# Stick-breaking attention: the causal table written into the scores by VectorE instead of added by TensorE

## The chip, the core and the metric

The kernel runs on one core of one Trainium2 chip. The metric is the device time of one execution in microseconds. TensorE (PE, with its weight loads as PEld), VectorE (DVE), ScalarE (ACT), GpSimd (POOL) and SyncE (SP) run their own instruction streams and wait for each other by semaphores.

## What is computed

Two transformer-like layers on 1024 tokens of width 1024 in float32. The first layer has a stick-breaking attention of 8 heads of width 128, a chunkwise retention of 4 heads, gates and projections; the second has gated linear attention, sliding-window attention and a feed-forward part. The change touches the stick-breaking attention alone:

```python
def block(args):                       # one tile of 128 queries
    z = einsum('bhqd,bhkd->bhqk', qi, k) * scale
    mask = kpos[None, :] < qpos[:, None]
    log_keep = where(mask, log_sigmoid(-z), 0.0)
    suffix = cumsum(log_keep, axis=3, reverse=True) - log_keep
    w = where(mask, exp(log_sigmoid(z) + suffix), 0.0)
    return einsum('bhqk,bhkd->bhqd', w, v)
```

## The kernel before

The program is one long sequence written by hand for each engine, without a scheduler: what an engine does next is the order of the lines in its block, and semaphores tie the engines together. The 30 projections come first (to about 653 us), then the stick-breaking attention (to about 1024 us), then branch projections, retention and the second layer.

**The attention stage.** `sb_pair(i, n)` runs for i = 0 to 3, each a pair of heads, and stands once in each engine's block. A pair has 16 steps S. `step(S)` gives head `c = S % 2` and a tile of 128 queries; `step_w(S)` gives the width, the keys up to and with the tile's own block. Even steps grow (S=0: 128, 2: 256, ... 14: 1024), odd steps shrink (S=1: 1024, 3: 896, ... 15: 128). The scores of step S lie in two PSUM banks, 4 and 5 or 6 and 7 by turns. One step goes over the engines so:

- PE `scores(S)`: the product of queries and keys in float32, up to 512 columns at a time (L2684; the trace shows each as two records), then on the last 128 columns the product of identity and table in fp32r (L2686), which adds -1e30 where a key isn't before its query. Then `z_done`. It first waits for `z_used` of step S-2, as the banks are shared.
- DVE `clamp(S)`: the smaller of score and 40 into `L` (L1943), then `m_ready`.
- ACT `softplus_terms(S)`: exp of L (L1343), relu of score less 40 into R (L1344), between them and the next the copy of the transposes of step S-2 (L1354), then a drain and ln of L (L1348), then `l_ready`.
- DVE `suffix_sum(S)`: scan from the right over L + R into C (L1951); `score_less_sum(S)`: a drain (L1956), then score less C into C (L1957), then `z_used`.
- ACT: exp of C (L1373), then `wgt`.
- PE `turn(S)`: transposes of C (L2695). ACT (L1354) and DVE (L1918) copy them out; `weigh` multiplies them with the values every two tiles (L2666), and DVE keeps that product (L1924).

The steps overlap. In iteration S VectorE runs: subtraction of S, copies of S-1 and of the values product, at S = 4, 5, 12, 13 half a weight block's low part (L1909), scan of S+1, clamp of S+2. ScalarE runs: exp of C for S, at times the copy of a gate product (L1365), the terms of S+2 with the copy for S inside. TensorE runs: the scores of S+2, part of the filler, the transposes of S, at some steps the values product, the rest of the filler. The filler (L2710) is the gate's projection in 512-column products, dealt out over the steps by a table (`fill_upto`), to give TensorE work while the chain of one step goes over the other engines. `end_of_pair` multiplies by the gate (L1936). Behind the last pair come the products of L593.

Near the kernel's start GpSimd loads the table `causal` by DMA, and ScalarE rounds it and the identity to fp32r (L1246, L1247), in place and into `ident_r`. PE waits for that before the stage (L2651).

Of the kernel before, what the change touches and what calls it, by code (L numbers as in the profile page):

```python
# [6 lines left out]
P = 128  # L7
KT = DM // P
TT = SEQ // P
# [50 lines left out]
def build(nc, x, norm_gain, w_in, b_merge, sb_q_gain, sb_k_gain, ret_out_gain, w_branch_sb, w_branch_ret, w_out,  # L60
          meta_tokens_2, norm_mix_w_2, w_in_2, w_gate_up_2, b_gate_2, gla_norm_w_2, sinks_2, w_out_2,
          norm_ff_w_2, w_ff1_2, w_ff2_2, final_norm_w_2, tab, out):
    f32, f32r, i32 = mybir.dt.float32, mybir.dt.float32r, mybir.dt.int32
    ACT, ALU, AX = mybir.ActivationFunctionType, mybir.AluOpType, mybir.AxisListType
# [5 lines left out]
    def at(name, shape, dt=f32, off=None):  # L70
        size = int(np.prod(shape[1:])) * 4
        o = cur[0] if off is None else off
        t = nc.alloc_sbuf_tensor_at(name, shape, dt, offset=o)
        if off is None:
            cur[0] += size
        return t

    ident = at("ident", [P, P])
# [21 lines left out]
    pos = [0]  # L100

    def work(name, shape, dt=f32):
        t = at(name, shape, dt, off=pos[0])
        pos[0] += int(np.prod(shape[1:])) * 4
        assert pos[0] <= work_end, (name, pos[0] - work_end)
        return t
# [29 lines left out]
    Q = work("q", [P, 2, SEQ])  # L136
    K = work("k", [P, 2, SEQ])
# [4 lines left out]
    WT = [work(f"wt{u}", [P, TT, 2 * P]) for u in range(2)]  # L142
    stage = [work(f"stage{u}", [P, HALF]) for u in range(2)]
    causal = work("causal", [P, P])
    causal_r = at("causal_r", [P, P], f32r, off=pos[0] - P * 4)
    ident_r = work("ident_r", [P, P], f32r)

    pos[0] = work_at
    S_hi = work("s_hi", [P, KT, SEQ], f32r)
# [96 lines left out]
    with ctx:  # L246
# [3 lines left out]
        def wide(b, w=SEQ):  # L250
            return ps[:, b:b + 2, :].rearrange("p a b -> p (a b)")[:, 0:w]
# [7 lines left out]
        const_in, const_ok = sem("constants_in"), sem("constants_ok")  # L259
# [356 lines left out]
        n1_hi, n1_lo, own_gain = sem("norm1_hi_and_raw_and_mask"), sem("norm1_lo"), sem("gain_in")  # L616
# [9 lines left out]
        z_done, m_ready, l_ready, z_used = sem("z_done"), sem("z_clamped"), sem("softplus_ready"), sem("z_used")  # L626
# [4 lines left out]
        causal_in = sem("causal_in")  # L631
# [540 lines left out]
        def _(act):  # L1172
# [68 lines left out]

            first_block(0)
            first_block(1)
            act.wait_ge(causal_in, 16)
            act.wait_ge(const_in, 16 * (1 + len(spec)))
            act.activation(causal_r[:, :], causal[:, :], ACT.Copy)  # L1246
            act.activation(ident_r[:, :], ident[:, :], ACT.Copy).then_inc(n1_hi, 1)  # L1247
            first_block(2)
            token_sum_hi(2, 4)
            first_block(3)  # L1250
# [521 lines left out]
        def _(dve):  # L1772
# [99 lines left out]
            for n in range(1, NPROJ + 1):  # L1872
# [17 lines left out]
                y, z = PC[out_tile(n, 3)][:, :], PC[out_tile(n, 2)][:, :]  # L1890
# [47 lines left out]
            def sb_pair(i, n):  # L1938

                def clamp(S):  # L1940
                    w = step_w(S % 16)
                    dve.wait_ge(z_done, 16 * i + S + 1)
                    dve.tensor_scalar(L[S % 2][:, 0:w], wide(4 + 2 * (S % 2), w), CLAMP, None, ALU.min).then_inc(m_ready, 1)  # L1943

                def suffix_sum(S):

                    w = step_w(S % 16)
                    dve.wait_ge(l_ready, 16 * i + S + 1)
                    if 16 * i + S >= 2:
                        dve.wait_ge(tr_done, 16 * i + S - 1)  # L1950
                    dve.tensor_tensor_scan(C[S % 2][:, 0:w][:, ::-1], L[S % 2][:, 0:w][:, ::-1], R[S % 2][:, 0:w][:, ::-1], 0.0, ALU.add, ALU.add)  # L1951

                def score_less_sum(S):

                    w = step_w(S)
                    dve.drain()  # L1956
                    dve.tensor_tensor(C[S % 2][:, 0:w], wide(4 + 2 * (S % 2), w), C[S % 2][:, 0:w], ALU.subtract).then_inc(z_used, 1)  # L1957

                if i == 0:
                    clamp(0)  # L1960
                    clamp(1)
                    suffix_sum(0)
                for S in range(16):
                    if S != 1 or i == 0:
                        score_less_sum(S)
                    if S - 2 in pair_after:
                        keep_attended(i, pair_after[S - 2])
                    if S >= 1:
                        keep_second(i, S - 1)
                    elif i:  # L1970
                        keep_attended(i - 1, 6)
                        keep_second(i - 1, 15)
                    if S in (4, 5):
                        half_lo(n + 1, 1, S - 4)
                    if S in (12, 13):
                        half_lo(n + 2, 0, S - 12)
                    if i < 3 or S < 15:
                        suffix_sum(S + 1)
                    if S == 0 and i:
                        score_less_sum(1)  # L1980
                        end_of_pair(i - 1)
                    if i < 3 or S < 14:
                        clamp(S + 2)
                if i == 3:
                    keep_attended(3, 6)
                    keep_second(3, 15)

            for i in range(4):
                sb_pair(i, L1 + 2 * i)
            end_of_pair(3)  # L1990
# [567 lines left out]
        def _(pe):  # L2558
# [70 lines left out]
            for n in range(1, NPROJ):  # L2629
# [18 lines left out]
                    pe.wait_ge(t_dve, 10)  # L2648
                product(n, 5)
                product(n, 6)  # L2650
            pe.wait_ge(n1_hi, TT + 5)  # L2651

            def weigh(i, q):

# [15 lines left out]
            def sb_pair(i, n):  # L2670

                def scores(S):
                    c, qt = step(S % 16)
                    w = step_w(S % 16)
                    if S % 16 == 0:
                        pe.wait_ge(qk_in, 32 * (i + S // 16) + 32)
                    if S % 16 == 1:
                        pe.wait_ge(v_in, 48 * (i + S // 16) + 32)
                    if 16 * i + S >= 2:
                        pe.wait_ge(z_used, 16 * i + S - 1)  # L2680
                    for h in range(0, w, HALF):
                        e = min(w, h + HALF)
                        z = wide(4 + 2 * (S % 2))[:, h:e]
                        pe.matmul(z, Q[:, c, qt * P:(qt + 1) * P], K[:, c, h:e], start=True, stop=(e < w))  # L2684
                    z = wide(4 + 2 * (S % 2))[:, w - P:w]
                    pe.matmul(z, ident_r[:, :], causal_r[:, :], start=False, stop=True).then_inc(z_done, 1)  # L2686

                def turn(S):
                    pe.wait_ge(wgt, 16 * i + S + 1)
                    if i or S:  # L2690
                        pe.wait_ge(wt0, 16 * i + S)
                    if i or long_steps(S):
                        pe.wait_ge(wt1, 8 * i + long_steps(S))
                    for kb in range(step(S)[1] + 1):
                        last = pe.transpose(wide(0)[:, kb * P:(kb + 1) * P], C[S % 2][:, kb * P:(kb + 1) * P], ident[:, :])  # L2695
                    last.then_inc(tr_done, 1)

                def filler(first, upto):

                    for m in range(first, upto):  # L2700
                        J, r = divmod(m, PASSES)
                        b, j = divmod(J, 4)
                        th, ct = j // 2, j % 2
                        k, g = divmod(r, 3)
                        if r == 0 and (i or J):
                            pe.wait_ge(g_raw, 8 * i + J)
                        if r == 0 and j == 0:
                            pe.wait_ge(w_lo, n + (1 + b))
                        w, a = ((W_hi, A_hi), (W_hi, A_lo), (W_lo, A_hi))[g]
                        last = pe.matmul(bank[3], w[b][:, k, ct * P:(ct + 1) * P], a[:, k, th * HALF:(th + 1) * HALF],  # L2710
                                         start=(r == 0), stop=(r == PASSES - 1))
                        if r == PASSES - 1:
                            last.then_inc(gp_done, 1)

                if i == 0:
                    scores(0)
                    scores(1)
                    pe.wait_ge(*v_kept(NPROJ - 1))
                else:
                    weigh(i - 1, 7)  # L2720
                for S in range(16):
                    first, upto = fill_upto[S - 1] if S else 0, fill_upto[S]
                    early = first if S - 1 in fill_after else upto if S == 0 else (first + upto) // 2
                    if S == 0:
                        filler(first, early)
                    if i < 3 or S < 14:
                        scores(S + 2)
                    if S:
                        filler(first, early)
                    elif i == 0:  # L2730
                        pe.wait_ge(*c_kept(NPROJ - 1, 3))
                    turn(S)
                    if S - 1 in pair_after:
                        weigh(i, pair_after[S - 1])
                    filler(early, upto)
# [534 lines left out]
```

## Time and profile before

| | |
|---|---|
| median of 3 runs | 2576.06 us (2573.29 to 2579.47) |
| the profiled execution | 2574.54 us |
| its span | 2572.8 us |
| PE busy | 2476.6 us, 96% |
| DVE busy | 1585.9 us, 62% |
| ACT busy | 1078.1 us, 42% |
| POOL busy | 213.3 us, 8% |
| chain that ended last | PE 79%, DVE 8%, ACT 5%, DMA 3% |

The span is what the trace covers; 1.7 us lie around it. Busy time of TensorE counts overlapping, pipelined products, whose ends are modelled; so the starts of two neighbouring products tell what one costs, and its printed duration doesn't. "Idle before" in brackets behind a row of the timeline is the time in which that engine had nothing to run, and what ended it.

### The profile page before, as it was taken

Reading aid. Unit: us, or ns where it says so; the run is one execution under the profiler, and the core shown is the slowest. Engines: PE = TensorE matmul, PEld = TensorE weight load, DVE = VectorE, ACT = ScalarE, POOL = GpSimd, SP = SyncE. Lnnn points to the kernel's source line nnn. Section 1 sums busy time; section 2 is a strip of 40 time slices with the busy share of each in tenths; the row PEclk is TensorE's granted clock in tenths of the full one; section 3 lists DMA queues with packets and bytes.
Section 4 is the critical chain, followed back from the end, with each engine's and each line's share of the span. In section 5 each row is a group of like instructions: output and inputs, shape, how many; then the busy total and the mean of one; then the engine's idle time right before and its main releaser. Section 6 shows DMA issues by size and latency. Waiting matters only on the chain.

```text
span 2572.8 us, 30810 instructions
## 1 busy us (share of the span) xinstructions
PE 2476.6 (96%) x12198; PEld 2016.7 (78%) x12198; DVE 1585.9 (62%) x2033; ACT 1078.1 (42%) x1749; POOL 213.3 (8%) x351
## 2 busy tenths in 40 slices
PE   6999999999899999999999999999999999999997
PEld 5777888888677777878788776887777888888886
DVE  7666556555566665366652556046737776788779
ACT  6454322233566666322421436134525444443333
POOL 0001111111000000100011003000001211200000
PEclk9999999999999999999999999999999999999999
DMA  4222333333221121634133310110143444583432
GB/s 141 90 80 97 98 127 103 98 103 133 79 92 62 57 80 50 232 115 178 37 98 128 115 49 18 50 34 17 60 130 107 143 154 154 198 298 141 157 127 102
DMA packets 139145, 278.49 MB, mean 108 GB/s; under 512 B 16765, under 2 KB 91178, under 8 KB 132218
## 3 DMA queue, kind: packets, MB, share of 16 engines
q1 hardware_dynamic: 109354, 176.52, 20.7%
q0 software_dynamic: 29648, 100.00, 11.0%
q8 instruction: 97, 1.59, 0.3%
q14 instruction: 46, 0.38, 0.1%
HBM read 196.79 MB, written 79.69 MB: 107 GB/s over the span
## 4 chain that ended last, share of the span: by engine, by line
PE 79%; DVE 8%; ACT 5%; DMA 3%; DVEq 2%; issue 2%; ACTq 1%; SPq 0%; POOL 0%
PE ps L2612 32%; PE ps L593 11%; PE ps L3242 8%; PE ps L2862 6%; PE ps L2710 4%; PE ps L2666 2%; PE ps L587 2%; PE ps L2684 2%; PE ps L3136 1%; DVE c L1951 1%; PE ps L2926 1%; PE ps L2620 1%; PE ps L2847 1%; PE ps L2695 1%; PE ps L3121 1%
## 5 line engine op out<-in xcount | busy, mean ns | idle before, releaser
L1870 DVE TENSOR_TENSOR proj_out<-ps,proj_out 128x512 f32<-128x512 f32 x292 | 195.9, 686 | 253.5 <-PE ps L2612 248.2
L2612 PE MATMUL ps<-a_hi,pw_hi 128*128 128x512 f32 x528 | 213.7, 405 | 0.8 <-ACT proj_out L1234 0.8
L2612 PE MATMUL ps<-a_lo,pw_hi 128*128 128x512 f32 x528 | 205.8, 390 | 0.0
L2612 PE MATMUL ps<-t_hi,pw_hi 128*128 128x512 f32 x464 | 188.5, 406 | 0.0
L2612 PE MATMUL ps<-t_lo,pw_hi 128*128 128x512 f32 x464 | 180.9, 390 | 0.0
L573 DVE TENSOR_TENSOR w_lo<-w_raw,w_hi 128x2048 fp32r<-128x2048 f32 x28 | 64.1, 2289 | 124.1 <-ACT w_hi L569 118.7
L2612 PE MATMUL ps<-a_hi,pw_lo 128*128 128x512 f32 x352 | 137.6, 391 | 0.0
L569 ACT ACTIVATE w_hi<-w_raw 128x2048 fp32r<-128x2048 f32 x28 | 53.6, 1913 | 164.9 <-DMA w_raw<-in_w_out 65.8
L1951 DVE TENSOR_TENSOR_SCAN c<-l,r 128x128 f32<-128x128 f32 (+7 forms) x64 | 86.8, 1356 | 57.3 <-ACT l L1348 57.2
L2612 PEld LDWEIGHTS ps<-a_hi,pw_hi 128*128 128x128 f32 x528 | 99.1, 188 | 24.8 <-issue 5.0
L2612 PEld LDWEIGHTS ps<-a_lo,pw_hi 128*128 128x128 f32 x528 | 99.2, 188 | 23.8 <-issue 3.8
L1815 DVE TENSOR_TENSOR pw_lo<-pw_raw,pw_hi 128x512 fp32r<-128x512 f32 x176 | 113.1, 684 | 0.1
L3242 PE MATMUL ps<-ws_hi,hidden_hi 128*128 128x512 f32 x288 | 112.2, 390 | 0.5 <-DVE a_plain L2505 0.5
L3242 PE MATMUL ps<-ws_lo,hidden_hi 128*128 128x512 f32 x288 | 112.1, 389 | 0.0
L3242 PE MATMUL ps<-ws_hi,hidden_lo 128*128 128x512 f32 x288 | 112.1, 389 | 0.0
L2710 PE MATMUL ps<-a_hi,w_hi 128*128 128x512 f32 x256 | 107.8, 421 | 3.0 <-DVE w_lo L573 2.9
L1198 ACT ACTIVATE pw_hi<-pw_raw 128x512 fp32r<-128x512 f32 x132 | 73.5, 621 | 86.3 <-DMA pw_raw<-in_w_in 43.3
L2612 PEld LDWEIGHTS ps<-t_lo,pw_hi 128*128 128x128 f32 x464 | 87.2, 188 | 21.3 <-issue 3.8
L2612 PEld LDWEIGHTS ps<-t_hi,pw_hi 128*128 128x128 f32 x464 | 87.2, 188 | 21.2 <-issue 3.8
L2862 PE MATMUL ps<-w_hi,a_hi 128*128 128x512 f32 x256 | 102.1, 399 | 0.0
L2710 PE MATMUL ps<-a_hi,w_lo 128*128 128x512 f32 x256 | 101.8, 398 | 0.0
L2710 PE MATMUL ps<-a_lo,w_hi 128*128 128x512 f32 x256 | 101.0, 395 | 0.0
(493 smaller groups left out, 6598.6 us busy)
## 6 DMA issues: line engine op xcount, KB each, us to landing
pw_raw<-in_w_in SPq DMA_DIRECT2D x30, 1024.0 KB, 5.8
hidden_raw<-hidden_forms SPq DMA_DIRECT2D x28, 1024.0 KB, 4.8
projections<-proj_out POOLq DMA_DIRECT2D x88, 256.0 KB, 3.4
w_raw<-in_w_in SPq DMA_DIRECT2D x18, 1024.0 KB, 5.2
pw_raw<-in_w_ff SPq DMA_DIRECT2D x16, 1024.0 KB, 6.3
w_quarter<-in_w_ff SPq DMA_DIRECT2D x16, 1024.0 KB, 7.1
hidden_forms<-proj_out POOLq DMA_DIRECT2D x56, 256.0 KB, 3.5
hidden_forms<-nb POOLq DMA_DIRECT2D x56, 256.0 KB, 3.4
```

The source lines that it names most:

```text
L569: act.activation(W_hi[s][:, :, :], W_raw[s][:, :, :], ACT.Copy).then_inc(w_hi, 1)
L573: dve.tensor_tensor(W_lo[s][:, :, :], W_raw[s][:, :, :], W_hi[s][:, :, :].bitcast(f32), ALU.subtract).then_inc(w_lo, 1)
L587: last = pe.matmul(bank[banks[j]][:, r * BC:(r + 1) * BC], a[:, k, t:t + P], w[s][:, k, :], start=(k == 0 and g == 0), stop=(k == KT - 1 a ...
L593: last = pe.matmul(bank[banks[j]][:, :], w[s][:, k, ct * P:(ct + 1) * P], a[:, k, th * HALF:(th + 1) * HALF], start=(k == 0 and g == 0), s ...
L1198: last = act.activation(PWH[s][:, q, :, :], raw_part(s, q), ACT.Copy)
L1815: last = dve.tensor_tensor(lo_part(s, q), raw_part(s, q), PWH[s][:, q, :, :].bitcast(f32), ALU.subtract)
L1870: return dve.tensor_tensor(out_ap(n, j), product_bank(n, o), src, ALU.add)
L1951: dve.tensor_tensor_scan(C[S % 2][:, 0:w][:, ::-1], L[S % 2][:, 0:w][:, ::-1], R[S % 2][:, 0:w][:, ::-1], 0.0, ALU.add, ALU.add)
L2612: last = pe.matmul(product_bank(n, o), w, a[:, k0 + k, t], start=(k == 0 and g == 0), stop=(k == 3 and g == 2))
L2710: last = pe.matmul(bank[3], w[b][:, k, ct * P:(ct + 1) * P], a[:, k, th * HALF:(th + 1) * HALF], start=(r == 0), stop=(r == PASSES - 1))
L2862: last = pe.matmul(bank[row_bank(t)], a[:, kk, tok], half_rows(w[s])[:, k, :], start=(s == 0 and k == 0 and g == 0), stop=(s == 1 and k == ...
L3242: last = pe.matmul(bank[4 * ((g + 1) % 2) + t], a[u][:, k, tok], w[u][:, k, :], start=(k == 0 and v == 0), stop=(k == 3 and v == 2))
```

## The change

VectorE waits once for the table ahead of the stage. Ahead of each clamp it now copies the table into the last 128 score columns in PSUM, where the table is not zero (the table's own bits are the predicate), and drains. TensorE's product of identity and table is gone, and the last product of the scores counts up `z_done`. The two ScalarE copies and TensorE's wait for them are gone, with the tiles `causal_r` and `ident_r`. The whole diff:

```diff
--- before.py
+++ after.py
@@ -142,8 +142,6 @@
     WT = [work(f"wt{u}", [P, TT, 2 * P]) for u in range(2)]
     stage = [work(f"stage{u}", [P, HALF]) for u in range(2)]
     causal = work("causal", [P, P])
-    causal_r = at("causal_r", [P, P], f32r, off=pos[0] - P * 4)
-    ident_r = work("ident_r", [P, P], f32r)
 
     pos[0] = work_at
     S_hi = work("s_hi", [P, KT, SEQ], f32r)
@@ -1241,10 +1239,6 @@
 
             first_block(0)
             first_block(1)
-            act.wait_ge(causal_in, 16)
-            act.wait_ge(const_in, 16 * (1 + len(spec)))
-            act.activation(causal_r[:, :], causal[:, :], ACT.Copy)
-            act.activation(ident_r[:, :], ident[:, :], ACT.Copy).then_inc(n1_hi, 1)
             first_block(2)
             token_sum_hi(2, 4)
             first_block(3)
@@ -1940,6 +1934,8 @@
                 def clamp(S):
                     w = step_w(S % 16)
                     dve.wait_ge(z_done, 16 * i + S + 1)
+                    dve.copy_predicated(wide(4 + 2 * (S % 2))[:, w - P:w], causal[:, :].bitcast(i32), causal[:, :])
+                    dve.drain()
                     dve.tensor_scalar(L[S % 2][:, 0:w], wide(4 + 2 * (S % 2), w), CLAMP, None, ALU.min).then_inc(m_ready, 1)
 
                 def suffix_sum(S):
@@ -1985,6 +1981,7 @@
                     keep_attended(3, 6)
                     keep_second(3, 15)
 
+            dve.wait_ge(causal_in, 16)
             for i in range(4):
                 sb_pair(i, L1 + 2 * i)
             end_of_pair(3)
@@ -2648,7 +2645,6 @@
                     pe.wait_ge(t_dve, 10)
                 product(n, 5)
                 product(n, 6)
-            pe.wait_ge(n1_hi, TT + 5)
 
             def weigh(i, q):
 
@@ -2681,9 +2677,8 @@
                     for h in range(0, w, HALF):
                         e = min(w, h + HALF)
                         z = wide(4 + 2 * (S % 2))[:, h:e]
-                        pe.matmul(z, Q[:, c, qt * P:(qt + 1) * P], K[:, c, h:e], start=True, stop=(e < w))
-                    z = wide(4 + 2 * (S % 2))[:, w - P:w]
-                    pe.matmul(z, ident_r[:, :], causal_r[:, :], start=False, stop=True).then_inc(z_done, 1)
+                        last = pe.matmul(z, Q[:, c, qt * P:(qt + 1) * P], K[:, c, h:e], start=True, stop=True)
+                    last.then_inc(z_done, 1)
 
                 def turn(S):
                     pe.wait_ge(wgt, 16 * i + S + 1)
```

## Rows read from the trace of the kernel before

**Rows 1.** Busy by stretch: A:B, us, PE, PEld, DVE, ACT, POOL, clock, DMA, GB/s.
```profile
834.00:924.00 90.00, 86.36 (x411) 67.41 (x410) 57.96 (x72) 59.10 (x98) 2.25 (x5) 1.00 0.22 71
```

**Rows 2.** Who waited for whom, 834 to 924 us: total us, times, longest.
```profile
PE ps L2695 <- ACT c L1373: 2.9, 4, 1.2
```

**Rows 3.** Timeline (start, us, engine, line, tiles, [idle before]), pair's start to the scores of S=5.
```profile
851.80 0.43 DVE L1943 TENSOR_SCALAR l<-ps 128x256 f32<-128x256 f32 x1 [0.77 <-PE ps L2686]
...
854.25 1.07 DVE L1943 TENSOR_SCALAR l<-ps 128x896 f32<-128x896 f32 x1
...
854.61 1.09 PE L2695 MATMUL ps<-ident,c 128*128 128x128 f32 x8 [1.17 <-ACT c L1373]
...
858.66 2.02 DVE L1951 TENSOR_TENSOR_SCAN c<-l,r 128x896 f32<-128x896 f32 x1 [2.23 <-ACT l L1348]
...
860.60 0.53 DVE L1943 TENSOR_SCALAR l<-ps 128x384 f32<-128x384 f32 x1
...
861.23 1.09 DVE L1957 TENSOR_TENSOR c<-ps,c 128x896 f32<-128x896 f32 x1
...
862.38 1.13 PE L2684 MATMUL ps<-k,q 128*128 128x512 f32 x2 [0.17 <-DVE c L1957]
```

**Rows 4.** Timeline, to the transposes of S=7.
```profile
874.20 0.42 DVE L1924 COPY out_t<-ps 128x256 f32<-128x256 f32 x1 [2.71 <-PE ps L2666]
...
881.72 0.80 DVE L1943 TENSOR_SCALAR l<-ps 128x640 f32<-128x640 f32 x1
...
885.87 0.77 PE L2695 MATMUL ps<-ident,c 128*128 128x128 f32 x5 [0.40 <-ACT c L1373]
```

**Rows 5.** Timeline, to the transposes of S=11.
```profile
898.87 0.53 DVE L1943 TENSOR_SCALAR l<-ps 128x384 f32<-128x384 f32 x1
...
901.47 0.96 DVE L1951 TENSOR_TENSOR_SCAN c<-l,r 128x384 f32<-128x384 f32 x1 [1.02 <-ACT l L1348]
...
902.60 1.09 DVE L1943 TENSOR_SCALAR l<-ps 128x896 f32<-128x896 f32 x1 [0.17 <-PE ps L2686]
...
907.47 0.55 PE L2695 MATMUL ps<-ident,c 128*128 128x128 f32 x3 [0.88 <-ACT c L1373]
```

**Rows 6.** Timeline, S=14 to the next pair's first scores.
```profile
913.13 1.23 DVE L1943 TENSOR_SCALAR l<-ps 128x1024 f32<-128x1024 f32 x1 [0.52 <-PE ps L2686]
...
920.23 0.27 DVE L1943 TENSOR_SCALAR l<-ps 128x128 f32<-128x128 f32 x1
...
920.59 1.23 DVE L1957 TENSOR_TENSOR c<-ps,c 128x1024 f32<-128x1024 f32 x1
...
921.96 0.46 PE L2684 MATMUL ps<-k,q 128*128 128x128 f32 x2 [0.51 <-DVE c L1957]
```

**Rows 7.** Groups by line, 650 to 1060 us: busy us, mean ns, idle before.
```profile
L2686 PE MATMUL ps<-causal_r,ident_r 128*128 128x128 f32 x64 | 30.1, 470 | 0.0
```

**Rows 8.** Timeline of TensorE at S=6.
```profile
868.07 1.02 PE L2684 MATMUL ps<-k,q 128*128 128x512 f32 x2
...
868.50 0.59 PE L2684 MATMUL ps<-k,q 128*128 128x512 f32 x1
...
869.27 0.40 PE L2710 MATMUL ps<-a_lo,w_hi 128*128 128x512 f32 x1
...
869.50 0.39 PE L2710 MATMUL ps<-a_hi,w_lo 128*128 128x512 f32 x1
```

**Rows 9.** Groups by line and shape on VectorE: ns min/median/max; busy us, mean ns.
```profile
L2209 DVE COPY_PREDICATED ss<-window,ps x14: 731/746/749, 1538.1 to 1588.1; 128x512 f32<-128x512 int32 x14
...
L1957 DVE TENSOR_TENSOR c<-ps,c 128x512 f32<-128x512 f32 x2 | 1.4, 692 | 0.2
...
L1957 DVE TENSOR_TENSOR c<-ps,c 128x128 f32<-128x128 f32 x2 | 0.6, 292 | 0.2
```

**Rows 10.** Busy TensorE by stretch at the stage's start: PE, granted clock.
```profile
668.00:670.00 2.00, 0.00 (x0) 0.86 0.00 0
...
674.00:676.00 2.00, 2.00 (x11) 0.50 0.00 0
```

## The prediction

> **What bounds the kernel now.** I began with the page's busy shares and its chain: TensorE is busy for 96% of the span and holds 79% of the chain that ended last, while VectorE is busy for 62%. Taken alone that speaks for the change, since it takes work from the busiest engine. But a share is a mean over stages, and the change lies in one, the attention of four head pairs between 653 and 1024 us. The second view is the busy time by stretch. One pair takes about 90 us; in it TensorE is busy 86.4 us, VectorE 58.0 and ScalarE 59.1, at a full granted clock [rows 1]. TensorE is nearly full, but not quite, and the question of this case is what ends its idle time.
>
> The third view is who waited for whom in one pair. TensorE's transposes (L2695) waited 2.9 us in four places for ScalarE's exp of the weights (L1373) [rows 2]. These places are not noise: they come back at the same steps in each of the pairs. The fourth view, the timeline, shows what stands behind each. I name a step by S (0 to 15 in a pair); each goes scores (PE L2684, L2686), clamp (DVE L1943), exp, relu, ln (ACT), scan (DVE L1951), subtraction (DVE L1957), exp (ACT L1373), transposes (PE L2695). TensorE covers this latency with the gate product (L2710) and the values product (L2666), but not wholly:
> - Behind the pair's start it waits 1.17 us at the transposes of S=1 (854.61) and 0.17 us at the scores of S=5 (862.38) [rows 3].
> - 0.40 us at the transposes of S=7 (885.87) [rows 4].
> - 0.88 us at the transposes of S=11 (907.47) [rows 5].
> - 0.51 us at the next pair's first scores (921.96) [rows 6], and once more right behind them, at the transposes of S=14, which wait for the exp of the same difference.
>
> At these places TensorE isn't the bound; the chain through VectorE and ScalarE is, and VectorE's clamp, where the change adds its work, lies in it.
>
> **What is removed.** 64 products of identity and table [rows 7]. The mean of 470 ns in that row is a pipelined latency, not a cost; starts tell the cost. The scores of S=6 are two records, the first starting at 868.07 and the second at 868.50, so 0.43 us each, and they would be through by 868.93. A 512-column gate product takes 0.23 us from start to start (869.27 to 869.50), so the second one behind the scores would start at 868.93 + 0.23 = 869.16 if nothing lay between. It starts at 869.27 [rows 8]. One L2686 ahead of the gate product thus costs TensorE 0.11 us. Ahead of transposes, which are short themselves, I take about half, 0.06, an estimate. If TensorE were the bound everywhere, 64 of them would give back 4 to 7 us; that is the change's ceiling. The two ScalarE copies near the kernel's start lie beside VectorE's sums of the token halves, for which ScalarE waits right behind them, so I cost them at nothing; if that cover were gone they would be worth two operations of about 0.3 us, the size of the 128x128 row in [rows 9]. The wait of TensorE for them (L2651) and the new wait of VectorE for the table are long fulfilled at 650 us: nothing. SyncE's waits on the count of finished scores move with TensorE.
>
> **What is added.** Ahead of each clamp, on VectorE, one predicated copy of 128x128 into the scores, and a drain. No row shows this shape, nor a VectorE write to PSUM. The kernel's own predicated copies are 128x512 and take 746 ns, where a subtraction of 128x512 takes 692 and one of 128x128 takes 292 [rows 9]. That is (692-292)/384 = 1.04 ns an element, so 746 - 384 x 1.04 = 346 ns for the new one. The bounds: not under the 0.27 us of the clamp of 128x128 (920.23) [rows 6], which reads one tensor where the copy reads two, and not over 746 ns, the large one. I take 0.35 us, nearest to the row of its own kind. The drain is read off the neighbours: a clamp without one in front begins 0.08 us before the scan ahead of it ends (858.66 + 2.02 = 860.68 against 860.60), the subtraction behind a drain begins 0.10 us after the clamp ends (860.60 + 0.53 = 861.13 against 861.23) [rows 3]. The clamp now comes behind such a drain, so each step's clamp ends c = 0.35 + 0.09 = 0.44 us later (0.36 to 0.84 by the bounds).
>
> These rows show that an explicit drain costs 0.10 + 0.08 = 0.18 us of overlap [rows 3]. The Trainium skill (VectorE: DVE Perf Modes, "The DRAIN you can't avoid") says that the pipe is emptied after every VectorE operation anyway, so that chaining operations saves nothing. By that rule the explicit drain would be free; the trace speaks against it, and the sum goes by the rows.
>
> VectorE's own load stays far from the bound: 58.0 + 16 x 0.44 = 65 us in a pair of over 90 [rows 1]. What counts is how often c is in the chain between two places where TensorE has the lead. Pair by pair, on the rows of the pair from 834 to 924:
> - Pair start to the scores of S=5 [rows 3]. Scores of S=2, clamp of S=2 (851.80), exp, relu, ln, scan of S=2, clamp of S=3 (854.25), exp, relu, ln, scan of S=3 (858.66), clamp of S=4 (860.60), which stands ahead of the subtraction of S=3 (861.23), and the scores of S=5 wait for that (862.38). Three clamps: 3c. TensorE is already idle before it, so there is no slack. The 1.17 us at S=1 is inside: ScalarE's queue holds the exp of S=1 behind the ln of S=2, so it grows by 1c.
> - Values product to the transposes of S=7 [rows 4]. VectorE keeps the attended rows when that product is done (874.20), splits a weight block, scans S=6, then clamps S=7, and after the scan of S=7 clamps S=8 (881.72); the exp of S=7 stands behind S=8's terms on ScalarE. 2c.
> - Values product to the transposes of S=11 [rows 5]. From VectorE's copy of it over the clamps of S=11 (898.87) and S=12 (902.60). The scan between ends at 901.47 + 0.96 = 902.43, so by the overlap of 0.08 the clamp of S=12 could have begun at 902.35, some 0.26 us earlier than it does; it was TensorE's scores that it waited for. 2c - 0.26.
> - Scores of S=14 to the next pair [rows 6]. Clamp of S=14 (913.13), scan, clamp of S=15 (920.23), subtraction (920.59), scores of the next pair (921.96). 2c.
>
> Sum 9c - 0.26 = 3.70 us a pair. Against it stand the removed products that lie where TensorE leads: S=5 and 6 (0.18), S=10 (0.12), S=14 (0.06, since the scores are announced earlier), and the next pair's S=1 and 2 (0.18): 0.54 us. The others end in a place where TensorE then waits anyway. Net 3.16 us a pair, and four pairs, since the first pair's start has the same three clamps on its way (there inside TensorE's wait of [rows 10]) and the last ends the same way: +12.6 us. Behind the stage TensorE leads alone and the shift stays.
>
> **The sum.** The profiled run took 2574.5 us (span 2572.8), so it becomes 2587.1. It is 1.5 us below the median of the three; I put the forecast between 2587.1 and 2576.1 + 12.6 = 2588.7, at 2588.
>
> **The rivals.**
> - *TensorE is the bound after all (faster).* If VectorE's extra 0.44 us went into its own idle time everywhere, the 64 products of 0.06 to 0.11 us would come off, some 5 us: about 2571 us. For it: VectorE idles a third of the pair. Against it: TensorE's waits stand behind these very clamps. It decides only if c is below 3.2/36 = 0.09 us, since 36c - 3.2 is the balance; the shortest VectorE row is three times that. 4%.
> - *Largely absorbed (within 0.2%).* A shorter copy and a free drain (c near 0.2) and part of the nine clamps hidden behind ScalarE, whose queue orders several of the exps: about 2579. 9%.
> - *A free drain.* If the drain costs nothing beside a copy this short, c is 0.35 - 0.08 = 0.27 us, the balance 36 x 0.27 - 3.2 = 6.5 us, the time 2581 us from the profiled run's own. Against it: the 0.10 us behind the drain in [rows 3]. This is what the Trainium skill's rule above would give. 9%.
> - *The forecast.* c between 0.3 and 0.5 at nine clamps a pair: 2582 to 2591. 61%.
> - *A dearer copy.* If writing PSUM under a predicate costs as much as the large copy (c = 0.84) the balance is 36 x 0.84 - 3.2 = 27, 2603 us; halfway, c = 0.6, it is 18, 2594 us. At such c further places with under 1 us to spare (the scores of S=9, S=12 and S=14) begin to wait too. 10%.
> - *The clock.* At the stage's very start TensorE has no product at all from 668 to 670 us, and then runs at half clock, 1.2 GHz, still from 674 to 676 [rows 10]. The waits inside the pairs (up to 1.17 us) have left the clock at 1.00 [rows 1]. They grow to 1.7 us, and at the pair's end to some 2 us in two parts. If one such place a pair brought the clock down as there, each would cost up to half of some 6 us, 12 us in all on top of the 12.6: 2600 us. 7%.
>
> **Range and chances.** 2581 to 2595 leaves out the first two cases and half of the last two, about 2 in 10. The likeliest alone is 2585 to 2591. A change of under 0.2% (5 us) can't be told from none in this kernel, whose three runs lie 6 us apart. The free drain lies on that edge, and I count a third of it as within. Faster 4%, within 12%, slower 84%.
>
> **What would show it.** In the changed kernel: a new VectorE group of 64 predicated copies of about 350 ns; the clamp beginning 0.09 us after each; a pair's period of about 93 us instead of 90; TensorE's waits in a pair about doubled, at the same steps as before (1.6 at S=1; 1.0 at S=5; 0.40 + 2c + 0.18 for the two products that fall away on TensorE's side = 1.5 at S=7; 0.88 + 0.62 + 0.18 = 1.7 at S=11); a granted clock of 1.00; the stretches ahead of 653 and behind 1024 of the same length. A period of 88 to 89 would overthrow the chain; a period of 93 with another length of copy would mean that the count of clamps is wrong; a clock under 1.00 inside pairs would be the last rival.

## The result and the profile after

The changed kernel takes 2587.96 us in the median of its runs, against 2577.32 for the kernel before in the same comparison: ratio 1.0040, 95% interval 1.0027 to 1.0054. Measured once more beside the experiments it is 2587.34 against 2576.22, ratio 1.0048, interval 1.0033 to 1.0063. The change costs 10 to 11 us. One of the seven runs in the first comparison took 8491.07 us at a mean granted clock of 0.407, and the ratio leaves it out; without it the median is 2587.1. The profiled execution took 2584.05 us.

The first lines of its page, span and busy time by engine:

```profile
span 2582.3 us, 30807 instructions
PE 2470.1 (96%) x12134; PEld 2005.0 (78%) x12134; DVE 1604.3 (62%) x2097; ACT 1078.6 (42%) x1747; POOL 212.8 (8%) x351
```

TensorE has 64 products less and is busy 6.5 us less; VectorE has 64 operations more and is busy 18.4 us more; the span is 9.5 us longer. Nothing in these lines says that the trade is bad, except the span. In the changed file the copy is L1937, the clamp L1939, the scan L1947, the subtraction L1953, the scores L2680, the transposes L2690, the gate product L2705.

One pair of heads in the middle of the stage, as the busy time of one stretch (to set beside [rows 1]), the copies as a group by line with busy time and mean ns, and who waited for whom in that stretch (to set beside [rows 2]; the last fence has the waits at the scores before):

```profile
838.00:930.60 92.60, 85.34 (x392) 65.09 (x392) 62.58 (x89) 59.17 (x99) 2.16 (x4) 1.00 0.20 68
```

```profile
L1937 DVE COPY_PREDICATED ps<-causal 128x128 f32<-128x128 int32 x64 | 18.2, 285 | 22.0 <-PE ps L2680 21.6
```

```profile
PE ps L2690 <- ACT c L1367: 4.8, 4, 1.6
...
PE ps L2680 <- DVE c L1953: 2.4, 2, 1.4
```

```profile
PE ps L2684 <- DVE c L1957: 0.7, 2, 0.5
```

The pair takes 92.60 us in place of 89.91. TensorE's busy time in it fell by 1.0 us, and its waits at the transposes grew from 2.9 us to 4.8 [rows 2], those at the scores from 0.7 us to 2.4: 3.6 us of waits became 7.2. VectorE is busy 62.6 us of 92.6, far from full. The work taken off TensorE turned into waiting.

I measure a pair by the subtraction of S=14, the one of width 1024 that closes it, at the ends of the second and the third pair. Before, the later one starts at 920.59 [rows 6] and the earlier one here, 89.91 us ahead of it:

```profile
830.68 1.23 DVE L1957 TENSOR_TENSOR c<-ps,c 128x1024 f32<-128x1024 f32 x1
```

After:

```profile
837.99 1.23 DVE L1953 TENSOR_TENSOR c<-ps,c 128x1024 f32<-128x1024 f32 x1
...
930.59 1.23 DVE L1953 TENSOR_TENSOR c<-ps,c 128x1024 f32<-128x1024 f32 x1
```

The timeline of the stretch that [rows 3] shows of before, from the scores of S=2 to those of S=5:

```profile
858.98 0.30 DVE L1937 COPY_PREDICATED ps<-causal 128x128 f32<-128x128 int32 x1 [1.10 <-PE ps L2680]
859.35 0.42 DVE L1939 TENSOR_SCALAR l<-ps 128x256 f32<-128x256 f32 x1
...
861.20 0.69 DVE L1947 TENSOR_TENSOR_SCAN c<-l,r 128x256 f32<-128x256 f32 x1 [1.42 <-ACT l L1342]
861.80 0.28 DVE L1937 COPY_PREDICATED ps<-causal 128x128 f32<-128x128 int32 x1
...
862.15 1.09 DVE L1939 TENSOR_SCALAR l<-ps 128x896 f32<-128x896 f32 x1
862.16 1.09 PE L2690 MATMUL ps<-ident,c 128*128 128x128 f32 x8 [1.61 <-ACT c L1367]
...
868.53 0.27 DVE L1937 COPY_PREDICATED ps<-causal 128x128 f32<-128x128 int32 x1
...
868.88 0.56 DVE L1939 TENSOR_SCALAR l<-ps 128x384 f32<-128x384 f32 x1
...
869.53 1.09 DVE L1953 TENSOR_TENSOR c<-ps,c 128x896 f32<-128x896 f32 x1
...
870.68 0.70 PE L2680 MATMUL ps<-k,q 128*128 128x512 f32 x1 [1.02 <-DVE c L1953]
```

Before, the clamp of S=3 begins (854.25) some 0.08 us before the scan in front of it ends (853.64 + 0.69 = 854.33). Now the copy stands in that place (861.80, the scan ends at 861.89) and the clamp comes 0.35 us later (862.15). Three such copies lie on the way to the scores of S=5, and TensorE waits there 1.02 us instead of 0.17, at the transposes of S=1 1.61 us instead of 1.17 [rows 3]. The waits at the transposes of S=7 and S=11, which were 0.40 and 0.88 us before [rows 4, 5]:

```profile
894.83 0.77 PE L2690 MATMUL ps<-ident,c 128*128 128x128 f32 x5 [1.25 <-ACT c L1367]
...
916.76 0.55 PE L2690 MATMUL ps<-ident,c 128*128 128x128 f32 x3 [1.42 <-ACT c L1367]
```

### The profile page after: what moved, and what is told of

Read it like the earlier page. It is cut to its first block, busy times and chain, and to the rows that moved or that the text cites. A ratio compares the mean times of both kernels' runs of the same rounds, so it can differ in the third digit from the quotient of the medians.

```text
span 2582.3 us, 30807 instructions
## 1 busy us (share of the span) xinstructions
PE 2470.1 (96%) x12134; PEld 2005.0 (78%) x12134; DVE 1604.3 (62%) x2097; ACT 1078.6 (42%) x1747; POOL 212.8 (8%) x351
## 4 chain that ended last, share of the span: by engine, by line
PE 79%; DVE 8%; ACT 5%; DMA 2%; issue 2%; DVEq 2%; ACTq 1%; SPq 0%; POOL 0%
PE ps L2609 32%; PE ps L591 11%; PE ps L3237 9%; PE ps L2857 6%; PE ps L2705 3%; PE ps L2662 2%; PE ps L585 2%; DVE c L1947 2%; PE ps L3131 1%; PE ps L2680 1%; PE ps L2921 1%; DVE l L1939 1%; PE ps L2617 1%; PE ps L2842 1%; ACT l L1337 1%
## 5 line engine op out<-in xcount | busy, mean ns | idle before, releaser
L1947 DVE TENSOR_TENSOR_SCAN c<-l,r 128x128 f32<-128x128 f32 (+7 forms) x64 | 86.8, 1356 | 57.7 <-ACT l L1342 57.6
L2705 PE MATMUL ps<-a_hi,w_hi 128*128 128x512 f32 x256 | 112.3, 439 | 2.9 <-DVE w_lo L571 2.8
L2705 PE MATMUL ps<-a_hi,w_lo 128*128 128x512 f32 x256 | 103.4, 404 | 0.0
L2705 PE MATMUL ps<-a_lo,w_hi 128*128 128x512 f32 x256 | 102.1, 399 | 0.0
```

## The experiments

My theory: a VectorE operation costs the kernel its own length in the nine of sixteen steps whose clamp lies in a chain that ends in a wait of TensorE; in the seven others it is free; the removed products give back little, since most of them lie where TensorE then waits. The rivals: TensorE's load decides (and the loss has another cause); every step counts alike; the explicit drain is free; the loss is granted clock.

All the expectations speak of the steady pair, and a single pair repeats within 0.1 us as long as the granted clock stays at 1.00, where whole runs of one kernel spread over some 9 us. (The pairs that end second, third and fourth take 89.93, 89.91 and 89.96 us before; the 25 runs of the kernel before in one comparison lie between 2571.71 and 2581.09 us.) So the pair decides, and the times stand beside it. Each version was profiled once, the changed kernel twice.

### Add alone, take away alone

**Both.** TensorE's product stays, VectorE's part is added:

```diff
 dve.wait_ge(z_done, 16 * i + S + 1)
+dve.copy_predicated(wide(4 + 2 * (S % 2))[:, w - P:w], causal_r[:, :].bitcast(i32), causal_r[:, :].bitcast(f32))
+dve.drain()
 dve.tensor_scalar(L[S % 2][:, 0:w], ..., CLAMP, None, ALU.min).then_inc(m_ready, 1)
```

> The kernel before with VectorE's predicated copy and drain added, while TensorE's product of identity and table stays. Chain theory (nine clamps a pair lie where TensorE waits; each is late by the 0.35 us from the copy's start to the clamp's, plus 0.01 for the clamp itself): 36 x 0.36 - 1 = 12 us longer than before, the stage's steady pair 93.0 us; that is 2 us longer than the change, which also gains on TensorE. Load theory (only the busiest engine's load counts, and the change lost its time for another reason than VectorE's part): same time as before. Undisturbed by chance drops of the granted clock, which move a run by 1.5 us each.

```profile
837.77 1.23 DVE L1959 TENSOR_TENSOR c<-ps,c 128x1024 f32<-128x1024 f32 x1
...
930.91 1.23 DVE L1959 TENSOR_TENSOR c<-ps,c 128x1024 f32<-128x1024 f32 x1
```

A pair of 93.14 us, 3.23 more than before; 2590.72 us against 2576.26, ratio 1.0051 (1.0036 to 1.0067). VectorE's part costs by itself more than the whole change does.

**No mask.** The changed kernel without copy and drain; it leaves the causal table out of the computation:

```diff
-dve.copy_predicated(wide(4 + 2 * (S % 2))[:, w - P:w], causal[:, :].bitcast(i32), causal[:, :])
-dve.drain()
```

> The changed kernel without the predicated copy and its drain: nobody masks the scores, so the causal table is left out of the computation. Chain theory: only the products that lie where TensorE leads come back, 0.54 us a pair and 2.2 us in all; a steady pair takes 89.4 us. If TensorE were the bound everywhere, the 64 products would give back 4 to 7 us, a pair 88.5 us.

```profile
830.37 1.23 DVE L1951 TENSOR_TENSOR c<-ps,c 128x1024 f32<-128x1024 f32 x1
...
919.80 1.23 DVE L1951 TENSOR_TENSOR c<-ps,c 128x1024 f32<-128x1024 f32 x1
```

A pair of 89.43 us, 0.48 less than before. The time is 2571.99 against 2576.26, ratio 0.9985 (0.9975 to 0.9994); the interval holds the 2 us that the pairs tell. So even with VectorE's part at no cost, the removal is worth about a tenth of a per cent, and TensorE isn't the bound everywhere.

### The parts of VectorE's cost

**Drain alone**, on the kernel before:

```diff
 dve.wait_ge(z_done, 16 * i + S + 1)
+dve.drain()
 dve.tensor_scalar(...)
```

> The kernel before with an explicit drain ahead of each clamp and nothing else. By the rows of before a drain takes 0.18 us of overlap where VectorE comes straight from other work (S = 3, 4, 7, 8, 11, 15 in the chain; at 12 it eats the slack) and nearly nothing where it waited for the scores (2, 14): about 1.0 us a pair less 0.2, +3 us in all, a pair 90.8 us. If an explicit drain is free, because the pipe is emptied anyway: no change, a pair 89.9 us.

```profile
832.91 1.23 DVE L1958 TENSOR_TENSOR c<-ps,c 128x1024 f32<-128x1024 f32 x1
...
924.03 1.22 DVE L1958 TENSOR_TENSOR c<-ps,c 128x1024 f32<-128x1024 f32 x1
```

91.12 us, 1.21 more; I had expected 0.8 to 1.0. The pair shows that an explicit drain with nothing else is not free; over nine steps it is 0.13 us a step. Where VectorE comes straight from a scan it is more: from the scan's start to the clamp of S=3 it was 0.61 us (853.64 to 854.25), here 0.77 (855.98 to 856.75). And it costs something even where VectorE had waited for the scores, which I had put at nearly nothing: from the start of TensorE's last product to the clamp of S=2 0.45 us before (851.35 to 851.80) and 0.52 here (853.62 to 854.14), at S=14 0.66 and 0.73. The time of whole runs is 2578.58 against 2576.26, ratio 1.0004 (0.9995 to 1.0014), and four pairs of 1.21 us are 4.8 us, which lies above that interval. In the profile the last S=14 comes 4.6 us later than before (1015.15 against 1010.55) and the part behind it is 1.8 us shorter; the code there is the same, and what shortens it is not shown.

The Trainium skill's section that I weighed in the prediction (VectorE: DVE Perf Modes, "The DRAIN you can't avoid") says that the pipe is emptied after every VectorE operation. My conclusion from it, that an explicit drain would then be free, doesn't hold here. The same section of the Trainium skill adds that a next operation that isn't held starts earlier. The trace agrees with that: without a drain the clamp of S=4 begins 0.08 us before the scan ahead of it ends [rows 3].

**Copy alone**, without the drain and into an unused tile of SBUF:

```diff
+scratch = [at(f"scratch{u}", [P, P], off=meta_at + u * KT * META * 4) for u in range(2)]
 ...
+dve.copy_predicated(scratch[S % 2][:, :], causal_r[:, :].bitcast(i32), causal_r[:, :].bitcast(f32))
 dve.tensor_scalar(...)
```

> The kernel before with the predicated copy of the table ahead of each clamp, but into an unused tile of SBUF and without a drain. Chain theory: each of nine clamps a pair is late by 0.285 us less the overlap of 0.08, some 0.2 to 0.25 us: 36 x 0.22 - 1 = +7 us, a pair 91.6 us. If the copy costs its time only when it writes PSUM, less; if the load is what counts, no change.

```profile
834.00 1.23 DVE L1959 TENSOR_TENSOR c<-ps,c 128x1024 f32<-128x1024 f32 x1
...
925.52 1.23 DVE L1959 TENSOR_TENSOR c<-ps,c 128x1024 f32<-128x1024 f32 x1
```

91.52 us, 1.61 more; 2582.41 against 2576.26, ratio 1.0022 (1.0012 to 1.0031). Copy and drain by themselves make 1.61 + 1.21 = 2.82 of the 3.23 us that they cost together; no run splits the remaining 0.41. The copy took 292 ns into SBUF and 285 into PSUM, so writing PSUM is no dearer.

**Semaphore in place of the drain**, in the changed kernel:

```diff
-dve.copy_predicated(wide(4 + 2 * (S % 2))[:, w - P:w], causal[:, :].bitcast(i32), causal[:, :])
-dve.drain()
+dve.copy_predicated(wide(4 + 2 * (S % 2))[:, w - P:w], causal[:, :].bitcast(i32), causal[:, :]).then_inc(masked, 1)
+dve.wait_ge(masked, 16 * i + S + 1)
```

> The changed kernel with a semaphore between the predicated copy and the clamp (the copy counts up, VectorE waits for the count) in place of the drain. From copy's start to clamp's start the drain version takes 0.35 us. If the wait for the finished copy costs as a drain does: a steady pair 92.6 us, no change. If the semaphore comes back some 0.05 us later than the drain lets go: 9 x 0.05 = 0.45 us a pair more, 93.0 us, +2 us in all.

Its timeline, a copy and the clamp behind it, and the pair:

```profile
858.76 0.28 DVE L1937 COPY_PREDICATED ps<-causal 128x128 f32<-128x128 int32 x1
859.07 1.09 DVE L1939 TENSOR_SCALAR l<-ps 128x896 f32<-128x896 f32 x1
```

```profile
834.98 1.23 DVE L1953 TENSOR_TENSOR c<-ps,c 128x1024 f32<-128x1024 f32 x1
...
927.22 1.22 DVE L1953 TENSOR_TENSOR c<-ps,c 128x1024 f32<-128x1024 f32 x1
```

I had the sign wrong: the semaphore lets the clamp go 0.31 us after the copy's start, the drain 0.35. Nine times 0.04 is 0.36, and the pair is 92.24, 0.36 shorter. The time, 2583.31 against 2576.06, ratio 1.0029 (1.0019 to 1.0039), lies 4 us below both measurements of the changed kernel, where four pairs give 1.4; the rest is not explained by the pairs.

### Which steps count

The masking is shared between the engines by a list of steps:

```diff
+MASK_BY_DVE = (...)
 ...
-pe.matmul(z, ident_r[:, :], causal_r[:, :], start=False, stop=True).then_inc(z_done, 1)
+if S % 16 not in MASK_BY_DVE:
+    last = pe.matmul(z, ident_r[:, :], causal_r[:, :], start=False, stop=True)
+last.then_inc(z_done, 1)
 ...
+if S % 16 in MASK_BY_DVE:
+    dve.copy_predicated(wide(4 + 2 * (S % 2))[:, w - P:w], causal_r[:, :].bitcast(i32), causal_r[:, :].bitcast(f32))
+    dve.drain()
```

**The nine steps in the chain**, (2, 3, 4, 7, 8, 11, 12, 14, 15):

> VectorE masks only at the nine steps a pair that the prediction counted in the chain (S = 2, 3, 4, 7, 8, 11, 12, 14, 15); at the other seven TensorE's product stays. Chain theory: nearly the whole loss of the change and a little more, since the gain at S = 1, 5, 6 and 10 is gone: 36 x 0.36 - 1 - 0.5 = +11.5 us on before, a steady pair 92.9 us. If every step counts alike, 9/16 of the change's 10 us: +6 us, a pair 91.4 us.

```profile
838.48 1.22 DVE L1961 TENSOR_TENSOR c<-ps,c 128x1024 f32<-128x1024 f32 x1
...
931.39 1.23 DVE L1961 TENSOR_TENSOR c<-ps,c 128x1024 f32<-128x1024 f32 x1
```

**The seven others**, (0, 1, 5, 6, 9, 10, 13):

> The counterpart: VectorE masks only at S = 0, 1, 5, 6, 9, 10, 13, where the prediction found slack, and TensorE's product stays at the nine others. Chain theory: nothing is lost and the products of S = 1, 5, 6 and 10 are gained, 0.42 us a pair: -1.7 us on before, a steady pair 89.5 us; the fastest version by the theory. If every step counts alike, 7/16 of 10 us: +4.4 us, a pair 91.1 us.

```profile
832.75 1.23 DVE L1961 TENSOR_TENSOR c<-ps,c 128x1024 f32<-128x1024 f32 x1
...
922.40 1.23 DVE L1961 TENSOR_TENSOR c<-ps,c 128x1024 f32<-128x1024 f32 x1
```

92.91 us for the nine and 89.65 for the seven: 3.00 more and 0.26 less than before, and 3.00 - 0.26 = 2.74 is within 0.05 of the 2.69 of the whole change. The two runs move TensorE's product along with VectorE's copy, so 0.26 is what the seven products give back less what the seven copies cost. An equal share for each step (91.4 and 91.1) is out. The times are 2594.3 against 2576.22, ratio 1.0069 (1.0054 to 1.0084), and 2575.21, ratio 0.9997 (0.9987 to 1.0007). The first is some 6 us more than four pairs of 3.00 us account for. Between the ends of its first and second pair the granted clock drops (below), and in its profile the part behind the last S=14 is 5.5 us longer than before (1567.79 us against 1562.25), though the code there is the same. One more drop of the clock stands in it, at 1026 to 1032 us; the rest is not accounted for.

**Two of the four chains alone**, S = 2, 3, 4 and S = 11, 12, one execution each:

> VectorE masks only at S = 2, 3, 4 of a pair, TensorE's product stays at the 13 others. The count says that all three lie in one chain, from the pair's first waits to the scores of S = 5: 3 x 0.36 less 0.06 for the scores of S = 2 being announced earlier, a steady pair 89.9 + 1.0 = 90.9 us. If they ran beside each other or had slack, 90.3 us (one of them) or no change. By an equal share of all sixteen steps 3/16 of 2.7: 90.4 us.

```profile
833.35 1.23 DVE L1961 TENSOR_TENSOR c<-ps,c 128x1024 f32<-128x1024 f32 x1
...
924.30 1.23 DVE L1961 TENSOR_TENSOR c<-ps,c 128x1024 f32<-128x1024 f32 x1
```

> VectorE masks only at S = 11 and 12. The count says two clamps in one chain, with 0.26 us of slack between them: 2 x 0.36 - 0.26 = 0.46 us, a steady pair 90.4 us. Without that slack 90.6 us; if the wait at S = 11 hung on TensorE's scores of S = 12 alone (one clamp), 90.2 us.

```profile
831.49 1.23 DVE L1961 TENSOR_TENSOR c<-ps,c 128x1024 f32<-128x1024 f32 x1
...
921.85 1.23 DVE L1961 TENSOR_TENSOR c<-ps,c 128x1024 f32<-128x1024 f32 x1
```

90.95 and 90.36 us: 1.04 and 0.45 more, against 1.0 and 0.46. The times of the two executions are 2587.0 and 2578.03 us against 2576.06. The first is 11 us longer than before, where four pairs make 4.2: its part behind the last S=14 takes 1569.94 us against 1562.25, with the same code. So here too the pair shows what the edit does and the whole time doesn't. Even the slack of 0.26 us between the clamps of S=11 and S=12, read off one row, is there.

### The dose, and the clock

**Double**: copy and drain twice ahead of each clamp.

```diff
+dve.copy_predicated(wide(4 + 2 * (S % 2))[:, w - P:w], causal[:, :].bitcast(i32), causal[:, :])
+dve.drain()
```

> The changed kernel with copy and drain twice ahead of each clamp. Chain theory: another 36 x 0.37 = 13 us on the changed kernel, a little more where further steps lose their slack; a steady pair 96 us. If VectorE's time were mostly hidden and the loss had another cause: no change.

```profile
847.14 1.23 DVE L1955 TENSOR_TENSOR c<-ps,c 128x1024 f32<-128x1024 f32 x1
...
944.87 1.22 DVE L1955 TENSOR_TENSOR c<-ps,c 128x1024 f32<-128x1024 f32 x1
```

97.73 us, 5.13 more than after, where nine steps of 0.37 us would give 3.3; 2607.9 us against 2576.22, ratio 1.0124 (1.0107 to 1.0141). The second dose costs 1.6 times the first. Its waits in a pair count five at the scores, where the changed kernel has two:

```profile
PE ps L2692 <- ACT c L1367: 5.2, 4, 2.0
PE ps L2682 <- DVE c L1955: 5.1, 5, 2.1
```

The three new waits are at the scores of S=9, S=12 and S=14, 0.65, 0.31 and 0.23 us: the very steps that the prediction names, as having under 1 us to spare, for a dearer copy. And the clock is in it. The stretches of its second, third and fourth pair, the granted clock behind TensorE's busy time:

```profile
757.00:850.00 93.00, 82.83 (x372) 0.98 0.20 66
850.00:947.00 97.00, 86.81 (x391) 0.99 0.20 66
947.00:1042.00 95.00, 88.80 (x390) 0.96 0.13 45
```

Before had 1.00 there. In stretches of 2 us the clock is down to 0.50, 1.2 GHz, at five places between 748 and 976 us, one of them (848 to 854) in the pair measured here.

**The changed kernel again.**

> The changed kernel once more, beside the others on one chip: +10 to +12 us on before, a steady pair 92.6 us. One point is open: its first profile had a stretch of half clock at the end of the first pair, 1.5 us long in effect. If that is chance, the pair boundaries of this profile need not have it; if the longer waits cause it, it is there again.

92.62 us a pair in the middle, as in the first profile. The open point is in both profiles: from the end of the first pair to the end of the second it is 94.18 and 94.20 us, 1.6 more than from the second to the third. The stretches of the first profile there, and one of the next pair's start, which has no drop:

```profile
744.00:748.00 4.00, 2.28 (x13) 0.92 0.31 120
748.00:752.00 4.00, 4.00 (x12) 0.65 0.17 66
752.00:758.00 6.00, 6.00 (x28) 1.00 0.00 0
...
838.00:842.00 4.00, 2.10 (x14) 1.00 0.34 119
```

Behind a stretch in which TensorE worked 2.28 of 4 us the clock falls (0.65 is a mean over 4 us at the two levels), and 1.6 us are lost. At the next pair's start it worked 2.10 of 4 us, and the clock stayed up. The nine steps have the longer pair there too (94.51 us), the version with both doesn't (93.13), though its pair is longer; its drop comes at the end of the fourth pair:

```profile
1028.00:1030.00 2.00, 2.00 (x8) 0.50 0.34 131
```

All profiles together, in stretches of 2 us from 690 to 1034 us: no stretch under 1.00 in the seven versions whose pair takes 91.12 us or less (before, no mask, drain alone, the seven others, the two single chains, the last version below), and at least one drop in the six whose pair takes 91.52 us or more: one each with copy alone, the semaphore and both, two with the nine steps, one and two in the two profiles of the changed kernel, five with the double dose. But for the double dose they all stand at the end of the first or of the fourth pair. So the drops come with the longer waits; which pair's end gets one isn't settled.

### A version that beats both

The semaphore's 0.31 us and the cost of the drain alone point to the stage's own drains, ahead of ln on ScalarE and ahead of the subtraction on VectorE. In both places another operation usually stands between the one that must be finished and the one that needs it:

```diff
+MASK_BY_DVE = (0, 1, 5, 6, 9, 10, 13)
 ...
-act.activation(R[S % 2][:, 0:w], ..., ACT.Relu, bias=-CLAMP)
+act.activation(R[S % 2][:, 0:w], ..., ACT.Relu, bias=-CLAMP).then_inc(n1_turned, 1)
 ...
-act.drain()
+act.wait_ge(n1_turned, TT + 16 * i + S + 1)
 act.activation(L[S % 2][:, 0:w], L[S % 2][:, 0:w], ACT.Ln, bias=1.0).then_inc(l_ready, 1)
 ...
-dve.tensor_tensor_scan(C[S % 2]..., 0.0, ALU.add, ALU.add)
+dve.tensor_tensor_scan(C[S % 2]..., 0.0, ALU.add, ALU.add).then_inc(scanned, 1)
 ...
-dve.drain()
+dve.wait_ge(scanned, 16 * i + S + 1)
 dve.tensor_tensor(C[S % 2][:, 0:w], ..., ALU.subtract).then_inc(z_used, 1)
```

(`n1_turned` is a semaphore of the first norm that stands at 8 by then.)

> A version meant to beat both: VectorE masks only at S = 0, 1, 5, 6, 9, 10, 13, as in other_steps, and the stage's two standing drains are replaced by semaphores on the instruction that must be finished: ScalarE's drain ahead of ln waits for the relu's count, VectorE's drain ahead of the subtraction waits for the scan's count. Both are mostly fulfilled when reached, since another operation lies between. Chain theory: some 0.18 us for each ln and subtraction in the chain, as far as it has no slack: 3 at S = 5's scores, 2 at S = 7, 1 at S = 11, 2 at the pair's end, 1.4 us a pair on top of other_steps' 89.65: a steady pair 88.2 us, -7 us on before (2569). If the drains cost nothing there, 89.65 and -1 us.

```profile
828.34 1.21 DVE L1961 TENSOR_TENSOR c<-ps,c 128x1024 f32<-128x1024 f32 x1
...
916.41 1.22 DVE L1961 TENSOR_TENSOR c<-ps,c 128x1024 f32<-128x1024 f32 x1
```

```profile
853.60 0.90 ACT L1345 ACTIVATE r<-ps 128x896 f32<-128x896 f32 x1
854.39 0.59 ACT L1355 ACTIVATE wt<-ps 128x512 f32<-128x512 f32 x1
854.87 0.95 ACT L1349 ACTIVATE l<-l 128x896 f32<-128x896 f32 x1
```

88.07 us a pair; 2569.5 against 2576.13, ratio 0.9972 (0.9962 to 0.9983). The ln of S=3 now begins 0.11 us before the copy ahead of it ends (854.39 + 0.59 = 854.98 against 854.87), where with the drain it began 0.08 us behind that end. The same chain through which the change lost 10 us gives back 7 when the stage's own gaps in it are closed. Of the 1.84 us a pair, 0.26 are the seven others'; how the 1.58 divide between ScalarE's drain and VectorE's no run shows.

## Why the prediction was right, point by point

- **The direction and the place.** Right: TensorE's waits in [rows 3 to 6] were the place where VectorE's time counts. "Both" shows the loss without the gain, "no mask" the gain without the loss, and the split by steps shows that nine steps carry the loss, while the seven others lose less than their products give back.
- **The count of nine a pair, less 0.26.** Right. With the cost of a copy measured (0.35 us from its start to the clamp's, and the clamp itself 0.01 longer, so c = 0.36) it gives 9 x 0.36 - 0.26 = 2.98 us; the nine steps alone measured 3.00, and two of the four chains alone came out as counted.
- **The price of a copy.** Mis-sized: 0.346 us by a slope through the 128x512 rows, 0.285 measured. The subtraction of the same 128x128 shape, 292 ns in [rows 9], would have been the better neighbour: at this size the two operations cost the same, and the surplus of the large copies is not a fixed cost that a small one keeps. With 0.09 for the drain, c was 0.44 where 0.36 is measured, the lower end of the bounds given there.
- **The gain on TensorE.** 0.54 us a pair, 0.48 measured (no mask). The seven others gained 0.26 where I had 0.42.
- **A pair.** 93 us forecast, 92.60 measured; net 3.16 against 2.69, by the price of the copy.
- **The waits.** 1.6 and 1.0 us at S=1 and S=5, measured 1.61 and 1.02. This match is in part luck: with the measured c the same sums, 1.17 + c and 0.17 + 2c, give 1.53 and 0.89. They leave out the products that fall away there on TensorE's side; without mask, where only the products are gone, these two waits are 1.24 and 0.26 us, 0.07 and 0.09 longer than before. At S=7 and S=11 1.5 and 1.7, measured 1.25 and 1.42; with c = 0.36 the same sums are 1.30 and 1.52.
- **The sum.** The last pair's subtraction of S=14 starts at 1023.17 us, before at 1010.55: 12.6 us later, just what was forecast for the stage. But the parts differ, and 0.3 of it lies ahead of the stage: VectorE's last sum of the projections starts at 651.29 against 651.03. So no gain from the two ScalarE copies taken out near the kernel's start is visible, as costed. Three steady pairs would have brought 2.7 each and the first, with those 0.3, brought 3.1, 11 us together; the other 1.6 is the drop of the clock at the end of the first pair, which I had given to a rival. And behind the stage the profiled run wins back 3.1 us: from that subtraction to the end it takes 1559.13 us against 1562.25. The code there is the same. In the profile of before the granted clock dips to 0.91 in 1460 to 1480 us and to 0.91 and 0.74 in 1600 to 1640; after has one dip fewer. The kernel before, too, was measured 1.3 us longer in the comparison (2577.32) than in the three runs that the forecast started from (2576.06): 12 us were forecast and 10.6 measured. The closeness of 2588 to the measured 2588 is thus in part luck; what the steps bear out is 11 us.
- **The clock as a rival.** It was right in kind and small in size: once in the first profile and twice in the second, 1.6 us where it can be read off, not at every pair. With the double dose it is there in all three later pairs. The forecast granted clock of 1.00 held between the ends of the second and the fourth pair and failed at the end of the first.
- **The free drain and the absorbed case.** Out: the drain alone costs 1.21 us a pair.

## What to carry to other kernels

A busy share of 96% doesn't make an engine the bound at the place of the change. List its few waits in one period of the stage, follow each back to where it had the lead, and count how many of the touched operations lie on that way; price times count, with the price read from the changed kernel's trace and the sum written down before each run, gave nine variants here to within 0.4 us a period of 90. It failed for the semaphore, where the price itself had the wrong sign, and for the double copy (96 us against 97.73), where the dose left the range of the slack and the clock dropped. Where an engine must wait for its own result, look first whether another operation can stand between and a semaphore can take the drain's place.

## What the runs showed of the hardware beyond this

- A predicated copy of 128x128 float32 takes 285 ns into PSUM and 292 into SBUF, the same as a subtraction of that shape, while at 128x512 it takes 746 against 692 ns.
- An explicit drain ahead of a VectorE operation costs 0.16 us where the operation would have begun before the scan ahead of it ended (0.61 against 0.77 us from start to start), and 0.07 where VectorE had waited for TensorE (0.45 against 0.52). Waiting for a semaphore of the first operation is 0.04 us quicker than the drain (0.31 against 0.35 us from start to start behind a copy of 0.28).
- The granted clock dropped to 1.2 GHz for a few us between 690 and 1034 us only in the versions whose pair took 91.52 us or more, where a drop cost 1.6 us; a start of a pair with as little work of TensorE (2.10 of 4 us) passed without one. Behind the stage the profile of before has such dips too, and not all follow a wait: TensorE was busy throughout from 1604 to 1620 us, and from 1620 to 1640 the clock was 0.74 in the mean. The spread of the runs goes with the clock: the runs of the kernel before with a mean granted clock of 0.992 took 2571.7 to 2572.8 us, those with 0.986 or 0.987 took 2579.8 to 2581.1.
